# Five modulation vectors written to DRAM as rows turned by TensorE, and a later place for four of them

## The chip, the cores and the metric

The kernel runs on one core of one Trainium2 chip. Its time is the device time of an execution in microseconds; the figure used is the median of several runs.

## What is computed

The reference runs two blocks one after the other on a sequence of 512 tokens with 1024 channels, in float32.

```python
def first_block(x, c, ...):
    mod = silu(c) @ ada_w + ada_b
    shift, scale, gate = split(mod, 3)
    h = rms_norm(x, norm_pre_w) * (1 + scale) + shift
    z = h @ w_in                       # pooling branch and a gated linear recurrence (8 heads)
    y = concat([pool_out, hgrn_out]) @ w_out
    return x + gate * rms_norm(y, norm_post_w)

def second_block(x, c, ctx, c_ctx, ...):
    x, ctx = layer_norm(x), layer_norm(ctx)
    sh1, sc1, g1, sh2, sc2, g2 = split(silu(c) @ w_ada + b_ada, 6)
    # latents of context and sequence, rotary part, attention (8 heads), a 31-tap convolution
    y = concat([conv_out, attn_out]) @ w_o + b_o
    x_mid = layer_norm(ALPHA * x + g1 * y, ln1_g, ln1_b)
    f = conv_ffn(x_mid * (1 + sc2) + sh2, w_up, dw_w, dw_b, w_down, b_down)
    return layer_norm(ALPHA * x_mid + g2 * f, ln2_g, ln2_b)
```

What matters here is that some modulation vectors of length 1024 multiply or are added along the channels in a stage where the tokens lie on the partitions. There they are needed as a row that is repeated on all 128 partitions, while they are computed as columns: channel 128 j + p lies on partition p in column j of a 128x8 tile.

## The kernel before

The five engines each have a program of their own, written out in order, and wait for each other on named semaphores. The weights come as a stream of items through three buffers (RAW), which SP fetches. They are used in blocks numbered nb. For each block ScalarE casts the high part (WH, `split`), VectorE subtracts it for the low part (WL, `split`), and TensorE multiplies three times (high by high, high by low, low by high). There are four WH/WL pairs, so the cast of block nb + 4 can start only when TensorE has finished block nb, and every `split` in ScalarE's program is a place in a fixed queue: what stands before it holds it up. Some items of the stream are pieces of the modulation matrices instead; VectorE reduces them with its own dot operations ("dots") spread over the blocks.

The blocks around the change are: 32 to 53 for the pooling branch (with what is left of the recurrence), 54 to 71 for the output matrix of the first block (B_OUT = 54; 58 and 59 are the two small ones of the last pooling group, with out<-DH), 72 to 85 for the input matrix of the second block. Of these 76 is the rotary part of the latent, 77 to 79 are the query latent. Before block 67 TensorE transposes the context, and in blocks 68 to 71 it works token tile by token tile, so that it goes through all four blocks for each tile.

The vectors go through a DRAM tensor `vectors` of five rows (VEC). One is G1, the product of the first block's gate and norm_post_w. VectorE makes it ahead of block 54. ScalarE stores it after block 54's place in its program and two blocks later waits for that store and issues two loads that repeat the row on all partitions (G1R). The other four (M2[:, 16:24], BG, M2[:, 40:48] and BD) are made at block 62's place and stored by ScalarE at block 66's. Two of them are loaded again behind the attention (GOR, BOR), two ahead of the last matrix (ROWS). All stores are written with a DRAM access pattern in which consecutive elements of one partition are 128 elements apart. SP's queue holds the weight items, the first block's input in token order and, behind the item of block 67, the context (XC).

In TensorE's program PSUM tiles for small work come from four banks that are taken in turn (`take_aux`), each once its former tile has been read. An operation of TensorE that is a plain transpose is a matmul with the identity (IDN) as the moving operand.

In the profile's rows, the tile DH is a pooling tile, and PX holds the small column tiles, G1 and M2 among them. AT and KDT are the two halves of G1R, GP and HB hold the gates of the pooling branch, and PTA is scratch. Helpers record the operations, so L200 is every ScalarE copy, L207 every two-input VectorE operation, L186 every matmul, L194 every transpose, L182 and L183 every issue of a DMA.

Of the kernel before, what the change touches and what calls it, by code (L numbers as in the profile page):

```python
# [357 lines left out]
def build_in(nc, ctx, A, out, consts, masks):  # L358
# [30 lines left out]
    def col(name, j=0, n=1):  # L389
        return PC[:, COL[name] + j:COL[name] + j + n]  # L390
# [124 lines left out]
    def js(j):  # L515
        return slice(j * 128, (j + 1) * 128)
# [247 lines left out]
    def act_prog(e):  # L764
# [233 lines left out]
        def shifted(i):  # L998
# [3 lines left out]
            a.act(XLT[:, i, :], XLT[:, i, :], ACTF.Identity, bias=R3[:, i:i + 1], scale=R2[:, i:i + 1])\  # L1002
                .then_inc(S_.a_s, ("u", i))

        for nb in range(B_OUT, B_OUT + 14):
            if nb in (B_OUT + 9, B_OUT + 10):
                for i in range(2):
                    y_squares(2 * (nb - B_OUT - 9) + i, 0)
            if nb not in (B_OUT + 4, B_OUT + 5):
                split(nb + NW)  # L1010
            if nb == B_OUT:
                tail(0, 1)
                a.wait_ge(S_.v_s, "g1")
                a.dma(VEC[0].rearrange("(j p) -> p j", p=128), G1, True).then_inc(S_.vec, "g1", by=16)
            elif nb == B_OUT + 2:
                a.wait_ge(S_.vec, "g1")
                a.wait_ge(S_.p_sm, ("qs", 7))
                for c in range(2):
                    a.dma(G1R[c], VEC[0:1, 512 * c:512 * c + 512].partition_broadcast(128)).then_inc(S_.row, *["g1"] * c, by=16)
            elif nb in (B_OUT + 4, B_OUT + 5):  # L1020
                pool_mix(0, nb - B_OUT - 4, nb)
            elif nb in (B_OUT + 6, B_OUT + 7):
                i = nb - B_OUT - 6
                if i == 0:
                    a.wait_ge(S_.ctx, "ctx")
                    a.wait_ge(S_.v_h, ("mix", 1))
                    a.wait_ge(S_.v_s, ("ss", 7))
                a.wait_ge(S_.a_st)
                a.act(PTA[:, 0:D], XC[:, i, :], ACTF.Identity, scale=2.0 ** -10, acc=CST[:, i:i + 1]).then_inc(S_.a_st)
                a.wait_ge(S_.a_st)  # L1030
                a.act(PTA[:, 0:D], XC[:, i, :], ACTF.Square, scale=2.0 ** -5, acc=CST[:, 2 + i:3 + i])\
                    .then_inc(S_.a_st, ("cst", i))
            elif nb == B_OUT + 8:
                for i in range(2):
                    a.wait_ge(S_.v_s, "cm")
                    a.act(XC[:, i, :], XC[:, i, :], ACTF.Identity, bias=CST[:, 6 + i:7 + i], scale=CST[:, 4 + i:5 + i])\
                        .then_inc(S_.a_s, *["xcn"] * i)
            if nb in (B_OUT + 11, B_OUT + 12):
                for i in range(2):
                    a.wait_ge(S_.x[2 + i], "x2")  # L1040
                for i in ((0, 1) if nb == B_OUT + 11 else (2, 3)):
                    a.wait_ge(S_.a_st)
                    a.act(PTA[:, 0:D], XT2[:, i, :], ACTF.Identity, scale=2.0 ** -10, acc=MX[:, i:i + 1])\
                        .then_inc(S_.a_st, ("mx", i))
            if nb == B_OUT + 12:
                a.wait_ge(S_.v_ada, ("w_ada_2", 47, "c2"))
                a.wait_ge(S_.v_s, "bd")
                for n, cols in enumerate((M2[:, 16:24], BG, M2[:, 40:48], BD)):
                    a.dma(VEC[1 + n].rearrange("(j p) -> p j", p=128), cols, True).then_inc(S_.vec, *["g2"] * (n == 3), by=16)

        def ctx_tile(k):

# [67 lines left out]
        def latent(m):  # L1120

            split(77 + m + NW)
            a.wait_ge(S_.p_blk, 77 + m)
            a.copy(CQ[:, m, :], main.of(("cq", m))).then_inc(S_.a_ev, ("cq", m))
            a.wait_ge(S_.a_ev)
            if m > 1:
                a.wait_ge(S_.v_s, ("qa", 1))
            a.act(TMP[:, 512:1024] if m else TMP[:, 0:512], CQ[:, m, :], ACTF.Square).then_inc(S_.a_s, ("cqq", m))

        latent(0)  # L1130
        latent(1)
        for i, (lo, hi) in enumerate(((0, 512), (512, NKEY))):
# [223 lines left out]
    def dve_prog(e):  # L1356
# [215 lines left out]
        def with_dots(nb):  # L1572
            for t in range(4):
                for h, step in heads_at(nb, t) if nb < B_OUT else ():
                    hgrn(h, step)
                dots(nb, t)

        for h in range(2):
            mix_low(8 + h, XT[:, h, :])
        for nb in range(32, 36):  # L1580
# [18 lines left out]
            mix_low(8 + h, XT[:, h, :])  # L1599


        v.wait_ge(S_.v_ada, ("ada_w", 23, "c"))
        v.tt(G1, M1[:, 16:24], col("norm_post_w", 0, 8), MUL).then_inc(S_.v_s, "g1")

        def tile_done(name, i, h, first, second):

# [131 lines left out]
        def conv(place):  # L1738
            for j, k in CONV[place]:
                if k == 0:  # L1740
                    v.wait_ge(S_.v_ev, ("u2", j, 0))
                    op = v.ts(CV[:, j, :], VP[:, j, 0:S], col("conv_dw_w_2", j), col("conv_dw_b_2", j), MUL, ADD)
                else:
                    v.wait_ge(S_.v_cv, ("tap", j, k - 1))
                    op = v.stt(CV[:, j, :], VP[:, j, k:k + S], col("conv_dw_w_2", 4 * k + j), CV[:, j, :], MUL, ADD)
                op.then_inc(S_.v_cv, ("tap", j, k), *[("cv", j)] * (k == 30))
# [321 lines left out]
    def pe_prog(e):  # L2068
        pe = Eng(e)

        def take(name, at=None):
            bk = main.take(name, at)
            if main.before(name) is not None:
                pe.wait_ge(EV, main.before(name))
            return bk

        def take_aux(name, at=None):
            bk = aux.take(name, at)
            if aux.before(name) is not None:
                pe.wait_ge(AX, aux.before(name))  # L2080
            return bk
# [173 lines left out]
        def rows(bks, nb, xs, first, last, which=range(4), done=True):  # L2255

            wh, wl = WH[nb % NW], WL[nb % NW]
            pe.wait_ge(S_.v_w, nb)
            for q, (xh, xl, ready) in enumerate(xs):
                cs = slice(512 * q, 512 * q + 512)  # L2260
                pe.wait_ge(*ready)
                for i in which:
                    op = pe.mm3(bks[i], xh[:, js(i)], xl[:, js(i)], wh[:, cs], wl[:, cs], first and q == 0, last and q == 1)
            if done:
                op.then_inc(S_.p_blk, nb)
            return op
# [14 lines left out]
        def mixes(k):  # L2281
            return [(*mix_at(kk % 16), (S_.v_h, ("mix", kk % 16))) for kk in (k, k + 1)]

        ys = [take(("y", i, 0)) for i in range(3)] + [take_aux(("y", 3, 0))]
        at = aux.no[("y", 3, 0)]
        for n, k in enumerate((4, 6, 8, 2, 10, 12, 14, 0)):
            if n == 4:
                for m in range(2):
                    pool_mix(0, m, B_OUT + 4 + m)
            rows(ys, B_OUT + n + 2 * (n >= 4), mixes(k), n == 0, n == 7)  # L2290
        ys = [take(("y", 0, 1))] + [take_aux(("y", i, 1), (at + 4 - i) % 4) for i in (1, 2, 3)]
        for n in range(4):
            if n == 3:
# [54 lines left out]
        tiles(take(("kv", 1)), 75, hh, hl, (), 8)  # L2348
        tiles(take(("kr", 0)), 76, hh, hl, (), 8, part=False)
        tiles(take(("kr", 1))[:, 0:NCTX], 76, hch, hcl, (), 8)  # L2350

        def tick(k):
            if k == 1:
# [265 lines left out]
```

## Time and profile before

| | |
|---|---|
| median of 3 runs | 1203.27 us (1202.9 to 1203.66) |
| profiled execution | 1202.24 us |
| its span | 1200.4 us |
| mean granted clock of TensorE | 0.989 |
| TensorE matmul busy | 1142.4 us (95%) |
| VectorE busy | 859.1 us (72%) |
| ScalarE busy | 552.6 us (46%) |
| GpSimd busy | 159.9 us (13%) |
| DMA packets under 512 B | 7760 of 28307 |

The times in the rows are microseconds from the start of the span. A row of a timeline has the start, the duration, the engine, the line and operation, out<-in with shapes, and the count; where the engine stood idle before it, the length and what ended the wait stand in brackets. A matmul's end is modelled, so the distance between two starts tells more than its duration. "ACTq" and "SPq" rows are issues of DMAs by ScalarE and SP; they are no compute but take the queue's time.

### The profile page before, as it was taken

The page shows a single profiled execution, that of the slowest core. Times are in us where ns is not written, and L with a number is a line of the kernel's source. Part 1 is how long each engine was busy: PE and PEld are TensorE (multiplying, and loading weights), DVE is VectorE, ACT ScalarE, POOL GpSimd, SP SyncE. Part 2 cuts the span into 40 slices and gives each one's busy share as a digit, 9 for nine tenths or more (in the row PEclk, how much of TensorE's full clock was granted, in tenths as well). Part 3 has the DMA queues.
Part 4 walks back from the last instruction along what each step waited for, and adds up shares of the span by engine and source line. Part 5 has one row for each costly group of instructions (what it writes and reads, how often), then busy time and mean ns, then how long its engine had stood idle before and what let it go on. Part 6 is the DMA issues. An engine that isn't in the chain of part 4 may idle for free.

```text
span 1200.4 us, 14193 instructions
## 1 busy us (share of the span) xinstructions
PE 1142.4 (95%) x5548; PEld 932.2 (78%) x5548; DVE 859.1 (72%) x1346; ACT 552.6 (46%) x855; POOL 159.9 (13%) x179
## 2 busy tenths in 40 slices
PE   3979999999999999999999999998999999999996
PEld 2868888888788877888887766777888888888885
DVE  5788899999867783675789899586665656555236
ACT  4365545445623341776425665536544444442130
POOL 0044443244423200000100000100000000000001
PEclk9999999999999999999999999999999999999999
DMA  8833323323425576453111011111222322234201
GB/s 311 302 141 106 112 99 141 123 88 141 156 99 185 190 271 174 137 51 121 69 35 39 1 70 71 36 70 71 95 84 103 106 104 75 103 130 168 76 30 70
DMA packets 28307, 136.61 MB, mean 114 GB/s; under 512 B 7760, under 2 KB 8016, under 8 KB 14416
## 3 DMA queue, kind: packets, MB, share of 16 engines
q1 hardware_dynamic: 20448, 128.46, 30.6%
q10 hardware_dynamic: 7792, 7.25, 2.3%
q8 instruction: 44, 0.72, 0.3%
q14 instruction: 23, 0.19, 0.0%
HBM read 133.58 MB, written 2.12 MB: 113 GB/s over the span
## 4 chain that ended last, share of the span: by engine, by line
PE 58%; DVE 21%; ACT 8%; issue 5%; DMA 4%; POOL 3%; ACTq 0%; DVEq 0%; SPq 0%; POOLq 0%
PE PB L186 58%; DVE RAW L1382 3%; DVE WL L207 3%; ACT WH L200 3%; DVE CV L215 1%; DVE XL L215 1%; POOL PTA L207 1%; DVE AT L235 1%; DMA RAW<-in_wstream 1%; POOL UPA L207 1%; DVE SS L215 1%; DVE UPA L207 1%; DVE PTA L207 1%; DVE MPH L1382 1%; DMA XL<-in_xT 1%
## 5 line engine op out<-in xcount | busy, mean ns | idle before, releaser
L186 PE MATMUL PB<-HH,WH 128*128 128x512 f32 (+1 forms) x896 | 351.0, 392 | 4.6 <-DVE HL L207 1.7
L207 DVE TENSOR_TENSOR WL<-RAW,WH 128x1024 fp32r<-128x1024 f32 (+2 forms) x174 | 207.8, 1201 | 187.6 <-ACT WH L200 187.2
L186 PE MATMUL PB<-HH,WL 128*128 128x512 f32 (+1 forms) x896 | 341.5, 381 | 0.0
L186 PE MATMUL PB<-HL,WH 128*128 128x512 f32 (+1 forms) x896 | 340.7, 380 | 0.0
L200 ACT ACTIVATE WH<-RAW 128x1024 fp32r<-128x1024 f32 (+2 forms) x174 | 169.3, 979 | 298.6 <-PE PB L186 262.9
L186 PEld LDWEIGHTS PB<-HH,WH 128*128 128x128 f32 x896 | 170.1, 190 | 36.4 <-DVE HL L207 2.3
L186 PEld LDWEIGHTS PB<-HH,WL 128*128 128x128 f32 x896 | 169.6, 189 | 32.9
L186 PEld LDWEIGHTS PB<-HL,WH 128*128 128x128 f32 x896 | 170.0, 190 | 28.7 <-issue 0.5
L215 DVE SCALAR_TENSOR_TENSOR CV<-VP,PC,CV 128x512 f32<-128x512 f32 x120 | 86.7, 764 | 0.7
L207 POOL TENSOR_TENSOR PX<-PX,NPOW 128x2 f32<-128x2 f32 (+2 forms) x7 | 6.2, 891 | 483.4 <-DVE PX L207 437.1
L186 PE MATMUL PB<-WH,AH 128*128 128x512 f32 x176 | 68.5, 389 | 0.0
L186 PE MATMUL PB<-WL,AH 128*128 128x512 f32 x176 | 68.5, 389 | 0.0
L186 PE MATMUL PB<-WH,AL 128*128 128x512 f32 x176 | 68.5, 389 | 0.0
L1382 DVE CUSTOM_DVE_ANT_0 RAW<-RAW,CR,PC 128x1024 f32<-128x1024 f32 x48 | 63.5, 1341 | 0.0
L207 POOL TENSOR_TENSOR PTA<-HB 128x256 f32<-128x256 f32 (+1 forms) x53 | 46.6, 904 | 116.5 <-DVE HB L232 107.7
L201 ACT ACT_TABLE_LOAD x44 | 56.5, 1283 | 7.2 <-issue 6.5
L186 PE MATMUL PB<-WH,HH 128*128 128x512 f32 x128 | 53.5, 418 | 4.4 <-DVE WL L207 4.1
L186 PE MATMUL PB<-WL,HH 128*128 128x512 f32 x128 | 52.0, 406 | 0.0
L186 PE MATMUL PB<-WH,HL 128*128 128x512 f32 x128 | 51.6, 403 | 0.0
L207 POOL TENSOR_TENSOR UPA<-HB 128x256 f32<-128x256 f32 (+1 forms) x51 | 45.1, 908 | 44.9 <-DVE HB L232 39.9
L215 DVE SCALAR_TENSOR_TENSOR PTA<-PB,PC,PTA 128x511 f32<-128x511 f32 x66 | 49.2, 747 | 1.2
L186 PE MATMUL PB<-PTA,VG 128*128 128x512 f32 x96 | 49.3, 597 | 0.7 <-ACT PTA L201 0.6
(279 smaller groups left out, 1841.2 us busy)
## 6 DMA issues: line engine op xcount, KB each, us to landing
RAW<-in_wstream SPq DMA_DIRECT2D x108, 1024.0 KB, 4.8
RAW<-in_wstream SPq DMA_DIRECT2D x5, 768.0 KB, 4.2
RAW<-in_wstream SPq DMA_DIRECT2D x5, 512.0 KB, 3.4
XL<-in_xT SPq DMA_DIRECT2D x2, 1024.0 KB, 10.0
HB<-in_x SPq DMA_DIRECT2D x2, 1024.0 KB, 6.9
out<-XL SPq DMA_DIRECT2D x8, 256.0 KB, 2.0
ROWS<-in_rows ACTq DMA_DIRECT2D x3, 512.0 KB, 7.8
XC<-in_ctx SPq DMA_DIRECT2D x1, 1024.0 KB, 7.1
```

The source lines that it names most:

```text
L186: return self.put(lambda e: e.matmul(o, l, r, start=start, stop=stop, skip_group_check=skip))
L200: return self.put(lambda e: e.activation(o, i, f))
L201: return self.put(lambda e: e.activation(o, i, f, bias=bias, scale=scale))
L207: return self.put(lambda e: e.tensor_tensor(o, a, b, op))
L215: return self.put(lambda e: e.scalar_tensor_tensor(out=o, in0=a, scalar=s, in1=b, op0=o1, op1=o2))
L235: return self.put(lambda e: e.copy_predicated(o, mask, d))
L1382: v.put(lambda e: e.tensor_tensor_reduce(out=PROD if vec == "cc" else w, in0=w, in1=ROW[vec], scale=1.0, scalar=col(bias, j + i), op0=MUL, ...
```

## The change

The store of a vector with a scattered pattern is replaced by three steps: TensorE transposes the 128x8 columns into an 8x128 tile in PSUM, ScalarE copies it to SBUF, and the store writes 8 runs of 128 elements for each vector. G1's product is made ahead of block 32 in VectorE's program instead of ahead of block 54; its transpose stands behind TensorE's first output block, and its copy and store are where the store was. The four others are transposed behind block 76 and stored by ScalarE behind the cast of block 80, ahead of the query latent, in one DMA instead of four; their rows are gathered in the fourth tile of CV, so VectorE's convolution waits for the store before it first writes there.

```diff
@@ ScalarE's program
+        def vectors_out(name, n, rows, dst, done):
+            a.wait_ge(S_.p_sm, name)
+            a.copy(rows[0:8, 0:128 * n], aux.of(name)[0:8, 0:128 * n]).then_inc(S_.a_ax, name)
+            a.wait_ge(S_.a_ax, name)
+            a.dma(dst.rearrange("n (j p) -> j n p", p=128), rows[0:8, 0:128 * n].rearrange("j (n p) -> j n p", p=128))\
+                .then_inc(S_.vec, done, by=16)
+
             if nb == B_OUT:
                 tail(0, 1)
-                a.wait_ge(S_.v_s, "g1")
-                a.dma(VEC[0].rearrange("(j p) -> p j", p=128), G1, True).then_inc(S_.vec, "g1", by=16)
+                vectors_out("g1t", 1, DG, VEC[0:1], "g1")
...
-            if nb == B_OUT + 12:
-                a.wait_ge(S_.v_ada, ("w_ada_2", 47, "c2"))
-                a.wait_ge(S_.v_s, "bd")
-                for n, cols in enumerate((M2[:, 16:24], BG, M2[:, 40:48], BD)):
-                    a.dma(VEC[1 + n].rearrange("(j p) -> p j", p=128), cols, True).then_inc(S_.vec, *["g2"] * (n == 3), by=16)
...
+        vectors_out("g2t", 4, CV[:, 3, :], VEC[1:5], "g2")
         latent(0)
@@ VectorE's program
+        v.wait_ge(S_.v_ada, ("ada_w", 23, "c"))
+        v.tt(G1, M1[:, 16:24], col("norm_post_w", 0, 8), MUL).then_inc(S_.v_s, "g1")
         for h in range(2):
             mix_low(8 + h, XT[:, h, :])
...
-        v.wait_ge(S_.v_ada, ("ada_w", 23, "c"))
-        v.tt(G1, M1[:, 16:24], col("norm_post_w", 0, 8), MUL).then_inc(S_.v_s, "g1")
...
                 if k == 0:
+                    if j == 3:
+                        v.wait_ge(S_.vec, "g2")
@@ TensorE's program
+        def turned(name, *cols):
+            for n, z in enumerate(cols):
+                op = pe.tr(aux.of(name)[0:8, js(n)], z, IDN[:, :])
+            op.then_inc(S_.p_sm, name)
...
             rows(ys, B_OUT + n + 2 * (n >= 4), mixes(k), n == 0, n == 7)
+            if n == 0:
+                take_aux("g1t")
+                pe.wait_ge(S_.v_s, "g1")
+                turned("g1t", G1)
...
         tiles(take(("kr", 1))[:, 0:NCTX], 76, hch, hcl, (), 8)
+        take_aux("g2t")
+        pe.wait_ge(S_.v_ada, ("w_ada_2", 47, "c2"))
+        pe.wait_ge(S_.v_s, "bd")
+        turned("g2t", M2[:, 16:24], BG, M2[:, 40:48], BD)
```

## Rows read from the trace of the kernel before

**Rows 1.** The page's part 1: busy time, share of the span, instructions.

```profile
PE 1142.4 (95%) x5548; PEld 932.2 (78%) x5548; DVE 859.1 (72%) x1346; ACT 552.6 (46%) x855; POOL 159.9 (13%) x179
```

**Rows 2.** Waits of TensorE, 430 to 560: waiter, releaser, sum, times, longest.

```profile
PE PB L186 <- DVE WL L207: 3.5, 2, 2.1
PE PB L186 <- ACT CKV L200: 1.5, 1, 1.5
```

**Rows 3.** Timeline of TensorE at block 58, block 61 and block 71.

```profile
453.29 0.40 PE L186 MATMUL PB<-DH,WH 128*128 128x512 f32 x1
...
461.25 0.39 PE L186 MATMUL PB<-WH,HL 128*128 128x512 f32 x1
463.76 0.65 PE L186 MATMUL PB<-WH,HH 128*128 128x512 f32 x1 [2.13 <-DVE WL L207]
...
468.22 0.39 PE L186 MATMUL PB<-WH,HH 128*128 128x512 f32 x1
...
509.45 0.39 PE L186 MATMUL PB<-WH,HL 128*128 128x512 f32 x1
511.24 0.50 PE L186 MATMUL PB<-WH,HH 128*128 128x512 f32 x1 [1.40 <-DVE WL L207]
```

**Rows 4.** Windows of TensorE: stretch, length, busy (instructions), granted clock, DMA share, GB/s.

```profile
464.00:465.00 1.00, 1.00 (x3) 0.50 0.12 49
```

**Rows 5.** Timeline of ScalarE, 440 to 480.

```profile
448.05 0.39 ACTq L182 DMA_DIRECT2D vectors<-PX  x1
...
460.22 0.34 ACTq L183 DMA_DIRECT2D AT<-vectors  x1
460.58 0.76 ACTq L183 DMA_DIRECT2D KDT<-vectors  x1
461.39 1.06 ACT L200 ACTIVATE WH<-RAW 128x1024 fp32r<-128x1024 f32 x1 [11.46 <-issue]
```

**Rows 6.** Timeline of VectorE: G1, block 61's low half, two dots.

```profile
444.31 0.15 DVE L207 TENSOR_TENSOR PX<-PX,PC 128x8 f32<-128x8 f32 x1
...
462.48 1.23 DVE L207 TENSOR_TENSOR WL<-RAW,WH 128x1024 fp32r<-128x1024 f32 x1 [11.29 <-ACT WH L200]
...
471.89 1.28 DVE L1382 CUSTOM_DVE_ANT_0 RAW<-RAW,CR,PC 128x1024 f32<-128x1024 f32 x1
...
506.69 1.22 DVE L219 CUSTOM_DVE_ANT_0 HB<-HB 128x1024 f32<-128x1024 f32 x1
```

**Rows 7.** The critical chain, 430 to 800: start, length, what.

```profile
448.05 12.14 DMA vectors<-PX
...
474.01 7.13 DMA XC<-in_ctx
```

**Rows 8.** Timeline of ScalarE at the four other stores.

```profile
504.82 1.57 ACTq L182 DMA_DIRECT2D vectors<-PX  x2
...
506.42 2.40 ACTq L182 DMA_DIRECT2D vectors<-PX  x2
508.87 1.06 ACT L200 ACTIVATE WH<-RAW 128x1024 fp32r<-128x1024 f32 x1 [2.96 <-issue]
```

**Rows 9.** Groups of ScalarE by form: a copy from PSUM, count, busy, mean ns.

```profile
L200 ACT ACTIVATE KH<-PB 64x512 fp32r<-64x512 f32 x8 | 4.7, 592 | 2.8 <-PE PB L186 2.6
```

**Rows 10.** DMA issues of the page's part 6, and landing of the tensor vectors' DMAs.

```profile
out<-XL SPq DMA_DIRECT2D x8, 256.0 KB, 2.0
...
DMA to landing us min/median/max: 3.0/6.2/14.9
```

**Rows 11.** Timeline of TensorE at the transposes of the context.

```profile
498.33 1.91 PE L194 MATMUL PB<-IDN,XC 128*128 128x128 f32 x16
499.99 0.48 PE L186 MATMUL PB<-WH,MPH 128*128 128x512 f32 x1
```

**Rows 12.** Timeline of TensorE near block 32.

```profile
330.07 1.16 PE L186 MATMUL PB<-UPA 128*128 128x128 f32 x8 [1.29 <-DVE AT L235]
```

**Rows 13.** Timeline of ScalarE behind block 76.

```profile
573.44 1.06 ACT L200 ACTIVATE WH<-RAW 128x1024 fp32r<-128x1024 f32 x1 [5.97 <-PE PB L186]
580.22 1.06 ACT L200 ACTIVATE WH<-RAW 128x1024 fp32r<-128x1024 f32 x1 [5.72 <-PE PB L186]
```

## The prediction

> **What bounds the kernel now.** I began with the busy shares on the page [rows 1]. TensorE works for 95% of the span, so time is won only where TensorE stands still or runs at its lower clock. Next came the list of TensorE's own waits around the two places that the diff touches [rows 2]. It shows 3.5 us spent waiting for the low half of a weight block (DVE WL), in two waits. The timeline of TensorE places them [rows 3]: 2.13 us before 463.76 and 1.40 us before 511.24.
>
> The first wait costs more than its length. In regular running the matmuls start 0.227 us apart. The last one before the gap starts at 461.25, the first behind it at 463.76, so 2.51 - 0.23 = 2.28 us are lost. Behind the gap the granted clock is 0.50 (1.2 GHz) [rows 4], after TensorE had stood still for 2.13 us; by 468.22 it is back at the other level (2.4 GHz). From 463.76 to 468.22 there are 12 starts, in 4.46 us instead of 12 x 0.227 = 2.73 us, so 1.73 us more. Together this is **4.0 us**.
>
> Where it comes from is seen on ScalarE [rows 5]. It issues the store of G1 into the DRAM tensor at 448.05. It casts blocks 59 and 60, and then waits at the loads of G1R for the store to land. This takes until 460.2: the critical chain has the store as one piece of 12.14 us [rows 7]. Block 61's cast is queued behind and begins at 461.39. It could have begun when TensorE was done with block 57, which is when TensorE turns to the pool blocks (out<-DH), at 453.29 [rows 3]. VectorE makes the low half at 462.48 [rows 6], and TensorE starts at 463.76.
>
> The second wait: ScalarE issues four stores [rows 8], 1.57 us from 504.82 and 2.40 us from 506.42. The queue's own work takes this long because each of the four is scattered. Block 71's cast is behind them and begins at 508.87 instead of about 505.8, where TensorE is through with block 67 (18 matmuls of blocks 68 to 70 lie between that and 509.68, 18 x 0.227 = 4.1). TensorE's starts at 509.45 and 511.24 [rows 3] give 1.79 - 0.23 = **1.56 us** lost; no slow stretch follows.
>
> **The change, part by part.**
>
> *G1's store becomes rows.* TensorE transposes G1 behind block 54, which ends before 437, so ScalarE finds it ready. At 448.6, after tail(0,1), ScalarE copies 8x128 from PSUM and waits for its own copy. The nearest copy from PSUM, of four times the columns, takes 0.59 us [rows 9]; I take 0.3 for this one and 0.1 for the wait. The store is issued at about 449.1 with 8 runs of 512 B in place of 1024 elements of 4 B. Nothing in the trace is such a store. Its landing is bounded by the output's stores, 2.0 us for 256 KB [rows 10], and by the store that it replaces, 12.14 us [rows 7]. I take 3 us, since the runs of the former are the closer kind; a weight item is being loaded at that time. Then the wait of ScalarE ends at about 452, the two broadcast loads take 0.34 + 0.76 us of issuing [rows 5], and the cast of block 61 starts at 453.5. With 1.05 for the cast and 1.23 for the low half it is ready at about 456, and TensorE wants it at 461.5. So the store may land as late as 461.5 - 2.5 (cast, low half, signals) - 1.1 (issues) = 457.9 before TensorE waits: 8.8 us after it is issued. Gain 4.0.
>
> As a page on this: the Trainium skill's "DMA: Bandwidth & Descriptors" (the table of rules at its end) says that a non-contiguous last dimension becomes one descriptor per element and is to be rearranged, and its section on the anatomy of one DMA gives about 2 us as the fixed cost, most of it the receipt of the write. By that figure, as an estimate, the store would land near 451 and the gain would be the same 4.0; the 12.14 us of the scattered one agrees in kind [rows 7].
>
> *What is late next, between 461 and 511.* ScalarE and VectorE do the pool blocks 58 and 59 as soon as TensorE has them (455 to 462, from 463 to 470 before). The dots at 471.89 [rows 6] free the buffer behind which SP issues the context's load at 474.01 [rows 7]; they move ahead by about 8 us, and the load with them, landing near 473 instead of 481.14. ScalarE is then 4 us earlier against TensorE than before, on top of TensorE's own 4, so nothing that was in time becomes late.
>
> *Four stores leave ScalarE at 504.82.* Block 71's cast can start at 505.8 (old time), its low half is done by 508.1; VectorE is free for it at 507.84 at the latest, when its last dot ends [rows 6], which gives 509.1. TensorE wants it at 509.68. Gain 1.56, with a cover of 0.6 us; were VectorE's dots 1 us later, 0.4 of it would be lost.
>
> *Where these stores go.* Behind block 76 TensorE makes four transposes; ScalarE copies 8x512 (0.59 by the same row) and issues one store of 32 runs (0.4 to 1.6 us, the ends of the old issues). This stands between the cast at 573.44 and the one at 580.22, before which ScalarE has 5.72 us idle until TensorE is done with block 77 [rows 13]. It needs 0.6 + 0.1 + 1.6 = 2.3 at most: free, if the cover stays. The waits added: ScalarE waits for the transposes with latent(0) queued behind, about 0.6 us inside the same idle time; VectorE waits for the store before the first tap of conv j = 3, some 40 us later; the loads of GOR and BOR are at 767. A load of the weights by SP no longer shares the DMA engines with 4096 elements.
>
> *TensorE's new work.* 16 transposes with what follows take from 498.33 to 499.99 (next start) [rows 11], plus 0.08 for the wider step behind: 1.74 us, 0.11 each. So G1's single one costs 0.11 and g2's four 0.44. For coming in and going out of a small group I add 0.1 twice. Sum 0.75; bounds 0.52 (5 x 0.104, no edges) and 1.2 (each group pays once more the 0.27 us duration of a transpose). All of it is on the path: TensorE has no idle time after block 54 that it could use, once 463.76 is mended, and none behind 559.27. The banks of PSUM used after g1t and g2t shift by one; their former tiles were read long before, so no wait.
>
> *G1's product moves ahead of block 32.* One VectorE operation of 0.15 us [rows 6], now at about 326, where VectorE bounds: TensorE waits 1.29 us for it at 330.07 [rows 12]. Cost 0.15. At 444.31 it leaves VectorE where TensorE has no wait, so this gives nothing.
>
> **Sum:** -4.0 - 1.56 + 0.75 + 0.15 = **-4.7 us** (-4.9 to -4.2 by the bounds of TensorE's work). The profiled execution took 1202.24 us with a span of 1200.4. So 1195.7 of span and 1197.5 for the execution; the median of the runs is 1.03 above that execution, 1203.27, which gives **1198.6 us**.
>
> **Rivals.**
> (a) *The lower clock falls elsewhere.* An idle of 1.5 us near 559, behind ScalarE's copies of CKV [rows 2], passes at the full clock now. Moved by 5 us, it could be followed by a stretch like that of 463.76: 1.73 us. For: the fall there followed an idle not much longer. Against: the runs agree within 0.8 us. Result -4.7 + 1.7 = -3.0, 1200.3. The Trainium skill ("TensorE: Matmul & The Clock Gate", Part 1) says that the clock's decision runs free of the kernel, so such a shift is possible.
> (b) *The gain is given back.* If the context's load were still issued near 474 (SP's order, not the dots, holding it), ScalarE's chain would keep its time, and TensorE would start block 71 near 509.2 instead of 511.24: -2.0 + 0.9 = -1.1, 1202.2. Against: SP's issue follows the dots' end at 473.1 by 0.9 us.
> (c) *The change doesn't do what it says:* the store by rows lands after 8.8 us but before about 12, behind the weight load. Each us beyond 8.8 brings back 1 us of idle, and the clock's 1.73. At 10 us: -4.7 + 1.2 + 1.7 = -1.8, 1201.5.
> (d) *Slower.* The same store in eight streams behind the megabyte loads of SP, landing as late as the slowest DMA of this tensor now, 14.9 us [rows 10]: at 449.1 + 14.9 = 464.0, 3.8 later than now. TensorE would lose 4.0 + 3.8 at the first place: +3.8 - 1.56 + 0.9 = +3.1, 1206.4. It decides from a landing of about 12 us on. Against: the 256 KB stores land in 2.0 us.
>
> **Numbers.** Forecast 0.77, (a) 0.08, (b) 0.06, (c) 0.05, (d) 0.04. A measurement of this kernel tells 0.2%, 2.4 us, from no change. Faster: the forecast, (a), and a small part of (c): 0.85. Same: (b) and the rest of (c), 0.11. Slower 0.04. The range reaches 1.8 us below the forecast (TensorE's work at its lower bound, and up to 1 us if the idles at 511 to 560, which hang on ScalarE, shrink as well) and up to (a) with 0.5 us for the spread of the runs: 1196.8 to 1200.8.
>
> **What would show it.** Right: no idle of TensorE between 431 and the context's transposes; granted clock 1.0 throughout 440 to 500; the store of G1 landing within 4 us; the context's load issued near 466; no wait for WL at block 71; 5 more transposes of 0.27 us; a first difference between the traces of at most 0.4 us until block 54. Wrong: a wait of ScalarE for that store past 457.9, or a new half-clock stretch behind 500.

## The result, and the profile after

| | before | after |
|---|---|---|
| median of the runs | 1203.47 us (1202.9 to 1204.26, 4) | 1195.47 us (1194.97 to 1200.34, 4) |
| ratio, 95% interval | | 0.9941 (0.9921 to 0.996) |
| profiled execution, span | 1202.24, 1200.4 | 1200.34, 1198.5 |
| the same kernels timed again | 1202.31 (1199.34 to 1207.14, 12) | 1195.35 (1193.86 to 1197.98, 6) |

The change makes the kernel faster by 8.0 us; 4.7 were forecast, and 1195.47 lies 1.3 us below the low end of the range. The direction and the mechanism were right and the size was not. The profiled execution of after happened to be the slowest of its four, so its own time says little. The page of after, parts 1 and 3, to set beside [rows 1]:

```profile
PE 1142.8 (95%) x5553; PEld 932.8 (78%) x5553; DVE 859.4 (72%) x1346; ACT 553.8 (46%) x857; POOL 160.0 (13%) x179
...
DMA packets 23163, 136.61 MB, mean 114 GB/s; under 512 B 2576, under 2 KB 2872, under 8 KB 9272
```

TensorE has five instructions more (the transposes), ScalarE two (the copies). The same bytes go in 5144 fewer packets. The packets under 512 B fall from 7760 to 2576, by 5184; 5120 of these are the elements of the five scattered stores (5 x 1024).

TensorE's waits of after, 430 to 560 (waiter, releaser, sum, times, longest), which answer to [rows 2]:

```profile
PE PB L186 <- ACT CKV L200: 1.5, 1, 1.5
PE PB L194 <- ACT PTA L201: 0.9, 1, 0.9
PE PB L194 <- DVE XL L215: 0.8, 1, 0.8
PE PB L186 <- DVE HB L215: 0.6, 1, 0.6
```

The wait for WL, 3.5 us in two pieces before, is gone. The window of after at block 61 (stretch, length, busy of PE, PEld, DVE, ACT, POOL, granted clock, DMA share, GB/s) answers to [rows 4]:

```profile
460.00:465.00 5.00, 5.00 (x24) 4.14 (x23) 3.83 (x5) 1.76 (x3) 0.00 (x0) 1.00 0.45 177
```

TensorE is busy for all of it, at 2.4 GHz. ScalarE's timeline of after shows why, beside [rows 5]:

```profile
450.85 0.25 ACT L200 ACTIVATE DG<-PB 8x128 f32<-8x128 f32 x1
451.13 0.55 ACTq L183 DMA_DIRECT2D vectors<-DG  x1
451.72 1.37 ACT L200 ACTIVATE WH<-RAW 128x256 fp32r<-128x256 f32 x2 [0.62 <-ACT DG L200]
454.10 0.36 ACTq L183 DMA_DIRECT2D AT<-vectors  x1
454.48 0.45 ACTq L183 DMA_DIRECT2D KDT<-vectors  x1
455.58 1.06 ACT L200 ACTIVATE WH<-RAW 128x1024 fp32r<-128x1024 f32 x1 [2.49 <-PE PB L186]
```

The store of eight runs is issued at 451.13, and ScalarE goes on at 454.10. So it landed within 2.97 us (3 were taken; 12.14 before). Block 61's cast waits for TensorE and no longer for the store. TensorE is 2.08 us later at this point of the program than in the trace of before, of which 0.2 is the change's own work and 1.9 is not (below); less the 1.9 the cast starts at 453.7, where 453.5 was forecast.

The second place and the new place of the four vectors, ScalarE's timeline of after, beside [rows 8] and [rows 13]:

```profile
503.81 1.06 ACT L200 ACTIVATE WH<-RAW 128x1024 fp32r<-128x1024 f32 x1 [3.66 <-PE PB L186]
...
569.72 1.06 ACT L200 ACTIVATE WH<-RAW 128x1024 fp32r<-128x1024 f32 x1 [5.90 <-PE PB L186]
570.68 0.57 ACT L200 ACTIVATE CV<-PB 8x512 f32<-8x512 f32 x1
571.28 0.30 ACTq L183 DMA_DIRECT2D vectors<-CV  x1
576.95 1.06 ACT L200 ACTIVATE WH<-RAW 128x1024 fp32r<-128x1024 f32 x1 [5.70 <-PE PB L186]
```

Block 71's cast now has 3.66 us of idle time ahead of it. Behind block 76 the copy and the store take 0.9 us of an idle time of which 5.70 us remain.

**How the executions are compared.** TensorE runs the same matmuls in the same order in all these kernels, so the start of the n-th one in two traces can be subtracted; a step in that difference is a loss or a gain at that place. This table gives, for each traced execution, what TensorE lost ahead of and just behind block 61 and block 71. Its zero is the changed kernel: its three traces and that of the kernel with G1 alone agree there to 0.05 us, whatever else happened in them (4.04 us less than the first trace of before at block 61, 1.68 less at block 71).

| traced execution of the kernel before | time, us | idle before block 61 | lost there, clock included | idle before block 71 | lost there | both |
|---|---|---|---|---|---|---|
| the one of [rows 3] | 1202.24 | 2.13 | 4.0 | 1.40 | 1.7 | 5.7 |
| c_before | 1199.34 | 2.96 | 6.0 | 0 | 0 | 6.0 |
| c_before2 | 1200.26 | 2.9 | 5.9 | 0 | 0 | 5.9 |
| c_before3 | 1201.92 | 3.0 | 6.1 | 0 | 0 | 6.1 |
| c_before4 | 1200.58 | 3.03 | 6.1 | 0 | 0 | 6.1 |
| c_before5 | 1207.05 | 2.59 | 2.9 | 4.25 | 6.7 | 9.7 |
| c_before6 | 1203.97 | 3.02 | 4.9 | 1.77 | 3.7 | 8.6 |

The execution on which the prediction rested had the smallest loss of the seven. The mean is 6.9 us: 5.15 at block 61 and 1.72 at block 71. The changed kernel loses none of it and pays 0.6 for its transposes, so these traces account for 6.3 us of the 8.0.

The loss at block 71 goes with how long ScalarE's issue of the four stores takes, from the start of the first to the end of the last:

| traced execution | issue of the four, us | lost at block 71 |
|---|---|---|
| c_before4, c_before3, c_before, c_before2 | 2.42, 2.53, 2.76, 2.76 | 0 |
| the one of [rows 8] | 4.00 | 1.7 |
| c_before6 | 4.51 | 3.7 |
| c_before5 | 5.57 | 6.7 |

### The profile page after: what moved, and what is told of

Read it like the earlier page. It is cut to its first block, busy times and chain, and to the rows that moved or that the text cites. A ratio compares the mean times of both kernels' runs of the same rounds, so it can differ in the third digit from the quotient of the medians.

```text
span 1198.5 us, 14203 instructions
## 1 busy us (share of the span) xinstructions
PE 1142.8 (95%) x5553; PEld 932.8 (78%) x5553; DVE 859.4 (72%) x1346; ACT 553.8 (46%) x857; POOL 160.0 (13%) x179
## 2 busy tenths in 40 slices
DMA packets 23163, 136.61 MB, mean 114 GB/s; under 512 B 2576, under 2 KB 2872, under 8 KB 9272
## 4 chain that ended last, share of the span: by engine, by line
PE 64%; DVE 19%; ACT 6%; issue 4%; POOL 3%; DMA 3%; DVEq 0%; SPq 0%; ACTq 0%
PE PB L186 64%; DVE RAW L1385 3%; DVE WL L207 3%; ACT WH L200 2%; DMA RAW<-in_wstream 2%; DVE CV L215 1%; DVE XL L215 1%; DVE AT L235 1%; DVE UPA L207 1%; DVE SS L215 1%; POOL UPA L207 1%; POOL PTA L207 1%; DVE PTA L207 1%; DVE MPH L1385 1%; DMA XL<-in_xT 1%
```

## The experiments

No kernel here leaves out a part of the computation. A ratio is to the kernel before on the same chip, with its 95% interval.

**The two kernels again.** c_before and c_after are the kernel before and the changed one, without an edit.

> The kernel before, unchanged, as a yardstick for what varies by itself. Theory S (the 2.7 us by which the medians moved more than the traces account for are a matter of the first 50 us, whose clock varies from execution to execution): executions of this kernel scatter too, some 3 us below or above 1203, and a second profile shows another offset against the first before block 4, with the same two stalls of 2.1 and 1.4 us of TensorE behind it. Theory R (the scattered stores cost more in the timed executions than the two stalls of the profile): its times stay within 1202.5 to 1204.5.

> The changed kernel, unchanged. Its first profile began 2.1 us late against that of before, with half the clock from 33 to 47 us, and lost 1.3 us at half clock near 715. Theory S: a profile that starts like the one before has a span of 1195 to 1196.5, and the ratio of many runs comes out at about -5.3 us (0.9956). Theory R: the ratio stays at -7 to -8 us (0.9935 to 0.994), also for an execution that starts alike.

Measured: c_before 1202.31 (12 runs), 0.9997 (0.998 to 1.0015); c_after 1195.35 (6 runs), 0.9932 (0.991 to 0.9954). The gain repeats: 8.2 us against the 23 runs of before that were timed beside them (median 1203.57, from 1199.41 to 1206.75), 7.0 against the 12 of c_before. Neither theory holds whole. S was right that the kernel before scatters (three runs had lain within 0.8 us, these 23 lie over 7.3, and 35 on another chip over 12.0), and wrong on the ratio; R was right that the gain is 7 us or more, and wrong on the scatter.

**One part of the change alone.** G1 alone (its rows, its transpose, its earlier product; the four others left as scattered stores at block 66's place), and the four others alone.

```diff
@@ e_g1_only, against the changed kernel
+            if nb == B_OUT + 12:
+                a.wait_ge(S_.v_ada, ("w_ada_2", 47, "c2"))
+                a.wait_ge(S_.v_s, "bd")
+                for n, cols in enumerate((M2[:, 16:24], BG, M2[:, 40:48], BD)):
+                    a.dma(VEC[1 + n].rearrange("(j p) -> p j", p=128), cols, True).then_inc(S_.vec, *["g2"] * (n == 3), by=16)
...
-        vectors_out("g2t", 4, CV[:, 3, :], VEC[1:5], "g2")
...
-        turned("g2t", M2[:, 16:24], BG, M2[:, 40:48], BD)
@@ e_g2_only, against the changed kernel
-                vectors_out("g1t", 1, DG, VEC[0:1], "g1")
+                a.wait_ge(S_.v_s, "g1")
+                a.dma(VEC[0].rearrange("(j p) -> p j", p=128), G1, True).then_inc(S_.vec, "g1", by=16)
...
-                turned("g1t", G1)
```

> Only G1 goes by rows; the four others are stored scattered at block 66's place as before. By the terms of the prediction: the stall before block 61 and the slow stretch behind it go (-4.0), one transpose and the product's move cost 0.35: -3.7 us, and the wait of 1.4 us before block 71 stays if it hangs on the issues, or shrinks if it hangs on the context's load being early. Theory R: -5 or more.

> Only the four vectors go by rows, behind block 76; G1's store stays scattered and its stall of 2.1 us with it. By the terms: -1.56 + 0.55 = -1.0 us, and the two single changes sum to what both do together, -4.7 to -5.3. Theory R: -3 or more.

Measured: e_g1_only 1195.09 (6), 0.9929 (0.9906 to 0.9951), the same as the whole change. e_g2_only 1201.9 (12), 0.9981 (0.9963 to 0.9999). In the trace of the latter TensorE loses 6.7 us at block 61 (the scattered store lands after 13.1 us, the idle time is 3.63 us) and nothing at block 71. Against 1203.57 that is 8.5 us for G1 alone, where 3.7 were expected, and 1.7 for the four others, where 1.0 was. The two don't add up: the whole change gains no more than G1 alone.

So G1 alone brings the second gain too, though the four scattered stores still stand where they stood. ScalarE's timeline of e_g1_only:

```profile
496.33 1.01 ACTq L182 DMA_DIRECT2D vectors<-PX  x2
...
497.38 1.46 ACTq L182 DMA_DIRECT2D vectors<-PX  x2
501.23 1.06 ACT L200 ACTIVATE WH<-RAW 128x1024 fp32r<-128x1024 f32 x1 [3.81 <-PE PB L186]
```

The issues take 2.5 us and hurt nobody, since ScalarE then has 3.81 us to spare before block 71. Together that is room for 6.3 us of issuing, more than the longest seen, 5.57. It is that early because the context's load is issued at 465.62 and not at 474.01 [rows 7]. The second loss thus needed two things at once: a context that came late, which G1's wait had made, and issues that took 4 us or more. By this room, to remove either is enough. e_g2_only shows no loss at block 71 either, but neither do four of the seven traces of before, so its one trace doesn't prove it.

**The wait or the form?** G1's scattered store with time enough to land: the product ahead of block 32, the store ahead of block 48's recurrence. In the second kernel the four others are stored behind block 76, scattered as before. Neither has a transpose.

```diff
@@ e_g1_early_scattered, against the kernel before
         for p, nb in ((2, 36), (1, 42), (0, 48)):
+            if p == 0:
+                a.wait_ge(S_.v_s, "g1")
+                a.dma(VEC[0].rearrange("(j p) -> p j", p=128), G1, True).then_inc(S_.vec, "g1", by=16)
@@ e_all_scattered_moved, on top of it
-            if nb == B_OUT + 12:
...
+        a.wait_ge(S_.v_ada, ("w_ada_2", 47, "c2"))
+        a.wait_ge(S_.v_s, "bd")
+        for n, cols in enumerate((M2[:, 16:24], BG, M2[:, 40:48], BD)):
+            a.dma(VEC[1 + n].rearrange("(j p) -> p j", p=128), cols, True).then_inc(S_.vec, *["g2"] * (n == 3), by=16)
         latent(0)
```

> G1's product ahead of block 32 and its scattered store, unchanged in form, issued at block 48's place, about 50 us ahead of the wait; the four others as before; no transposes. Theory W (all of the gain is that ScalarE no longer waits for that store): the stall and slow stretch before block 61 are gone as with the rows, the second stall too since the context's chain is early; 1195 us like G1 alone by rows, 0.15 faster by the transpose. Theory F (the form matters, for 1024 elements of 4 B hinder the weight loads wherever they are): slower than G1 by rows by over 2 us, with waits for RAW near block 48.

> As the run before, and the four others scattered too, but issued behind block 76, where the rows' store of the changed kernel is: no transposes at all, 4 us of issuing in a gap of 5.7 us. Theory W: 0.6 us faster than the changed kernel (no transposes: 0.1 at block 54, 0.46 behind block 76), 1194.8. Theory F: slower than it, with a wait of TensorE for block 81's low half near 580.

Measured: 1204.59 (12), 1.0 (0.9982 to 1.0018), and 1206.01 (12), 1.0003 (0.9983 to 1.0023). Both are as slow as before, although in both the waits for WL at blocks 61 and 71 are gone and the 4.04 and the 1.68 us come back there. They are lost at a new place. Of e_g1_early_scattered, ScalarE's timeline:

```profile
414.38 0.39 ACTq L182 DMA_DIRECT2D vectors<-PX  x1
...
430.01 1.06 ACT L200 ACTIVATE WH<-RAW 128x1024 fp32r<-128x1024 f32 x1 [8.85 <-DMA RAW<-in_wstream]
```

its view of the tile RAW (the buffers of the weight stream), 405 to 460, last line, and TensorE's waits, 400 to 440:

```profile
DMA to landing us min/median/max: 2.9/5.8/12.7
```

```profile
PE PB L186 <- DVE HB L215: 6.9, 1, 6.9
```

Nobody waits for the store. But the weight item that is being loaded beside it takes 12.7 us (in the same stretch of after none takes over 7.5), ScalarE waits 8.85 us for it, TensorE 6.9, and 4.9 us at 1.2 GHz follow. By the difference of the matmuls' starts 8.6 us are lost between 430 and 455. In the second kernel the same load takes 12.8 us, and 9.0 are lost. Its four stores behind block 76 hold up a load too, which lands after 16.8 us, but cost TensorE nothing that the difference shows (no step between 560 and 600). So theory F came true for G1's store, and not for the four others: a load that is held up costs time only where its item is needed soon. In e_g1_only, too, the load beside the four stores takes 16.9 us, and TensorE loses nothing.

This was foreseen by no step of the prediction: **the scattered store holds up the megabyte loads beside it**, not only the engine that waits for it.

**Half of it.** Columns 0 to 3 of G1 stored early, 4 to 7 at the old place.

```diff
@@ e_g1_half, against the kernel before
+                a.dma(VEC[0, 0:512].rearrange("(j p) -> p j", p=128), G1[:, 0:4], True).then_inc(S_.vec, by=16)
...
-                a.dma(VEC[0].rearrange("(j p) -> p j", p=128), G1, True).then_inc(S_.vec, "g1", by=16)
+                a.dma(VEC[0, 512:1024].rearrange("(j p) -> p j", p=128), G1[:, 4:8], True).then_inc(S_.vec, "g1", by=16)
```

> Half of G1's columns stored scattered at block 48's place, the other half where the store was, so 512 elements are waited for instead of 1024. If the landing goes with the number of elements it is 6 to 7 us, inside the 8.8 us that TensorE's cover allows: no idle before block 61 and 1195 to 1196 us. If it has a large fixed part (12 us whatever the number) the stall stays and the time is near 1203.

Measured: 1210.97 (12), 1.0047 (1.0025 to 1.0069), slower than before. Neither 1195 nor 1203 came out. 512 elements do all that 1024 do: the load beside the early half takes 13.8 us and TensorE stands still for 8.0 us. That half lands after 11.4 us; the second, issued at 454.38, after 11.75 us, at 466.13. The time does not go with the number of elements. By the starts of the matmuls 8.9 us are lost ahead of block 54, 0.5 at block 61 and 5.6 at block 71: behind the first stall TensorE is so late that ScalarE's wait for the second half hardly matters at block 61, but the context's load is issued only at 480.05, and the four stores then stand in the way of block 71.

**Neither the wait nor the rows: the store alone.** To the changed kernel one more store of G1 is added, into a DRAM tensor of its own, right behind the row store. Nothing waits for it until 760. In e_extra_dense its elements lie side by side as in the kernel before; in e_extra_apart each of the 1024 lies at the start of a 512-byte row of its own. The diff is that of the former; in the latter SCR has the shape [D, 128] and the store goes to SCR[:, 0].

```diff
@@ against the changed kernel
+    SCR = nc.dram_tensor("extra", [D], F32).ap()
...
                 vectors_out("g1t", 1, DG, VEC[0:1], "g1")
+                a.dma(SCR.rearrange("(j p) -> p j", p=128), G1, True).then_inc(S_.extra, by=16)
...
         a.wait_ge(S_.p_sm, ("o", 7, 5))
+        a.wait_ge(S_.extra)
```

> The changed kernel with the old scattered store added back right behind the store by rows, into a DRAM tensor of its own and waited for only behind the attention. If the wait is the whole cost (theory W), same as the changed kernel within 0.5 us. If a scattered store holds up the DMAs beside it (theory F), the packets of 8 KB of the weight loads take over 2 us again, the loads of G1R and the cast of block 62 come late, and the kernel loses 2 to 6 us.

> As the run before, but each of the 1024 elements goes to a row of its own, 512 B apart. If the elements hinder each other because neighbours in DRAM come from different partitions, it lands within 3 to 5 us and disturbs nothing: same as the changed kernel. If the number of small writes is what counts, it is as slow as the dense one.

Measured: e_extra_dense 1200.91 (12), 0.9984 (0.9972 to 0.9997); e_extra_apart 1197.61 (11), 0.9955 (0.994 to 0.997). These two ran on another chip than c_after, where the kernel before has a median of 1202.9 and not 1203.57, so their distance from c_after is given by medians and by ratios. ScalarE's timeline of e_extra_dense:

```profile
451.23 0.40 ACTq L182 DMA_DIRECT2D extra<-PX  x1
...
466.61 1.06 ACT L200 ACTIVATE WH<-RAW 128x1024 fp32r<-128x1024 f32 x1 [8.27 <-DMA RAW<-in_wstream]
```

The last line of its view of the tile RAW, 405 to 460, and below it that of e_extra_apart:

```profile
DMA to landing us min/median/max: 3.0/4.8/14.0
```

```profile
DMA to landing us min/median/max: 3.0/4.9/7.5
```

The dense store takes back 5.6 us by the medians (1200.91 against 1195.35) and 6.3 by the ratios, as theory F expected. By the starts of the matmuls it is 1.1 us at block 62, whose weights came late, and 4.4 at block 65, whose cast stands in ScalarE's program behind the context's statistics: the context's load is issued at 475.69 here and at 468.19 in after. The dense store itself lands after 10.4 us, and the first load of G1R beside it takes 14.2 us and not 4.6. The store with its elements apart lands after 4.2 us and loses nothing at either place. Its median is 2.3 us above c_after all the same (2.8 by the ratios). Its trace is 1.0 us longer than c_after's, and 0.9 of that is there before 100 us, long before the store; whether the rest of the medians' distance is a cost is open.

The records of the DMA packets say the same. A packet of 8192 B of the weight stream usually takes 0.31 us. Behind the first 60 us of the span these many took over 2 us:

| kernel | scattered dense stores | packets over 2 us |
|---|---|---|
| before, seven traces | 5 | 59 to 76 |
| e_g1_half | 6, two of them with 512 elements | 85 |
| e_g1_early_scattered | 5 | 67 |
| e_all_scattered_moved | 5 | 32 |
| e_g1_only | 4 | 38 |
| e_g2_only | 1 | 33 |
| e_extra_dense | 1, not waited for | 35 |
| e_extra_apart | 1, elements 512 B apart | 4 |
| changed kernel, three traces | 0 | 0 |
| e_g2_early (below) | 0 | 0 |

The four of e_extra_apart took 2.00 to 2.05 us; the longest of the changed kernel took 1.66.
In the first trace of before the 1024 packets of G1's store all start between 450.85 and 451.93 and are recorded at 9 ns each, and yet the store has landed only at 460.2. The packets of 8192 B beside it take up to 3.7 us, up to 9.9 us in e_extra_dense.

As a page on this: the Trainium skill's "DMA: Bandwidth & Descriptors" (Specifications) gives 512 B as the least transfer for the line rate and says that below it the DMA engines read, modify and write. e_extra_apart, with just as many elements under 512 B and hardly a delay, shows that the size alone isn't it. What matters is that they lie densely in DRAM. Whether elements in the same few hundred bytes hinder each other, or all of them in the same 4 KB, was not tried, and the mechanism inside was not measured.

**The place of the four others.** The changed kernel with its four rows made early: transposed ahead of TensorE's work on the context, copied into DG and stored at block 66's place, where the scattered stores were.

```diff
@@ e_g2_early, against the changed kernel
             if nb == B_OUT + 12:
+                vectors_out("g2t", 4, DG, VEC[1:5], "g2")
...
         for n in range(4):
+            if n == 2:
+                take_aux("g2t", at)
+                pe.wait_ge(S_.v_ada, ("w_ada_2", 47, "c2"))
+                pe.wait_ge(S_.v_s, "bd")
+                turned("g2t", M2[:, 16:24], BG, M2[:, 40:48], BD)
```

> The changed kernel with the four vectors transposed ahead of block 66 and stored by rows at block 66's place, where the scattered stores were. The store's issue is one of 0.5 us instead of four with 4 us, and ScalarE has 3.7 us idle before block 71's cast in the changed kernel: nothing lost, same as the changed kernel within 0.3 us. Rival (the place behind the rotary latent is worth the 1.6 us of the second stall): 1.5 us slower, with a wait for WL before block 71.

Measured: 1201.79 (12), 0.9979 (0.9959 to 0.9999), 6.4 us above c_after by the medians and 5.7 by the ratios (another chip again). TensorE's waits of e_g2_early, 430 to 560:

```profile
PE PB L194 <- ACT DG L200: 2.6, 1, 2.6
...
PE PB L194 <- ACT XR L198: 1.3, 1, 1.3
```

and ScalarE's copy of the rows:

```profile
497.02 0.57 ACT L200 ACTIVATE DG<-PB 8x512 f32<-8x512 f32 x1
```

Here no low half comes late and nothing at block 71 waits. Of the four banks for small work the only one free for these rows is one that the context's transposes need soon after. TensorE waits 1.3 us until ScalarE has read the bank's former tile, and 2.6 us more at the context, until ScalarE has copied the rows, at 497.02: the copy stands at block 66's place in its program, 9 us behind the transposes. So 4.7 us are lost between 475 and 509 (the four transposes included, which are then missing behind block 76); the remaining 1 us or more of the medians' distance isn't seen in the trace. Both expectations missed. The later place matters, but not for the issues of the stores: it is a bank that is held until ScalarE comes to the copy in its queue.

**Does the loss at these two places go with the time of an execution?** Both kernels without an edit, one profiled execution each.

> The kernel before once more, one look. Its two traces so far lost 4.0 + 1.6 and 6.0 + 0.0 us before blocks 61 and 71 and came out at 1202.2 and 1199.3, both below the median of 1203.6 of its 35 executions. If the place before block 61 carries what the medians moved beyond the prediction, another execution shows a landing of 12 to 14 us and 4 to 8 us lost there, and its time goes with that.

> As the run before: the loss before block 61 lies between 4 and 8 us. If instead the executions differ in the first 100 us or behind 700, the loss before block 61 is 4 to 6 us again and the rest of the gain stays open.

> One more traced execution of the kernel before. If its time is above 1203.6, the loss before blocks 61 and 71 together is 8 us or more (the slow executions are slow there); the rival is 6 us there and the rest in half-clock stretches in the first 100 us or behind 700.

> As c_before4. Over the traced executions of before, the time goes with the loss before blocks 61 and 71 if that is the cause; by the rival it goes with what is lost in other stages.

> As c_before4: above 1203.6 with 8 us or more lost before blocks 61 and 71, or with 6 us there and the rest in other stages.

> A third trace of the changed kernel: no idle of TensorE between 431 and the context's transposes, no packet of a weight load over 2 us behind 60 us, 1194 to 1198 us; with a slow start like that of its first trace 1200.

Measured: 1200.26, 1201.92, 1200.58, 1207.05, 1203.97, and 1194.33 for the changed kernel; the losses stand in the table above. The two executions of before that are above its median are those with 8.6 and 9.7 us lost; the other five lost 5.7 to 6.1. The times less these losses still lie from 1193.3 to 1197.4, so other places scatter as much as these two. Of c_before5, TensorE's timeline:

```profile
463.33 0.50 PE L186 MATMUL PB<-WH,HH 128*128 128x512 f32 x1 [2.59 <-DVE WL L207]
...
512.07 0.79 PE L186 MATMUL PB<-WH,HH 128*128 128x512 f32 x1 [4.25 <-DVE WL L207]
```

its ScalarE's timeline:

```profile
504.09 1.46 ACTq L182 DMA_DIRECT2D vectors<-PX  x2
...
505.58 4.08 ACTq L182 DMA_DIRECT2D vectors<-PX  x2
509.70 1.06 ACT L200 ACTIVATE WH<-RAW 128x1024 fp32r<-128x1024 f32 x1 [4.53 <-issue]
```

and its windows behind the two places:

```profile
513.00:514.00 1.00, 1.00 (x4) 0.71 (x3) 0.17 (x1) 1.00 (x5) 0.00 (x0) 0.50 1.19 25
464.00:465.00 1.00, 1.00 (x6) 0.82 (x5) 0.36 (x1) 1.00 (x2) 0.00 (x0) 1.00 0.74 131
```

Here the issues of the four stores took 5.5 us and not 4.0 [rows 8], and TensorE stood still for 4.25 us before block 71. Behind it the starts come slowly for 4.8 us (11 of them), at 1.2 GHz. Behind block 61, after 2.59 us of idle time, the clock was 2.4 GHz in this execution; in c_before, after 2.96 us, 14 starts come at 1.2 GHz, in 6.0 us instead of 3.2; in the one of [rows 4], after 2.13 us, 12 in 4.46, of which 9 are slow. In c_before6, after 3.02 us of idle time, the first five come at 2.4 GHz and the next nine at 1.2. So such a stall costs about its own length, or up to 2.9 us more.

The rest of the scatter is seen in both kernels. In the first 100 us the seven traces of before differ by up to 2.0 us, the three of the changed kernel by up to 3.6. At 705 to 711 some lose 1.3 to 1.6 us, and others differ by 1.0 us near 775 and 1.5 near 822. Windows of after at two of these places:

```profile
706.00:707.00 1.00, 1.00 (x3) 0.33 (x1) 1.00 (x3) 0.51 (x2) 0.00 (x0) 0.50 0.00 0
40.00:45.00 5.00, 5.00 (x17) 4.32 (x18) 4.80 (x10) 1.38 (x2) 0.00 (x0) 0.50 0.82 306
```

That is why its profiled execution took 1200.34. It is 1.7 us late at 100 us, most of it from 39 to 42, at half clock, which the trace of before enters only at 40.7; 0.2 more come at a wait near 427, and 1.3 at 706, at half clock.

## Why the prediction was right in kind and too small

- **The first term, -4.0, is the step that failed.** The mechanism held (the store's landing, ScalarE's wait, block 61's cast, and half clock behind the stall). The size was that of one execution. Seven show 2.9 to 6.1 us there, with a mean of 5.15, and e_g2_only 6.7. The landing varied little (12.1 to 13.1 us); the clock's share behind it did, from nothing to 2.9 us. That makes 1.15 of the 3.3 us by which the forecast was too small.
- **The second term, -1.56,** has a mean of 1.72 over the seven, so its size was fair, but it is 0 in four of them and 3.7 and 6.7 in two. Its cause was half told. The prediction put it down to the issues, and it does go with their length; e_g1_only shows that with the context's load early they are harmless. That an issue takes long "because each of the four is scattered" is also only half of it: the one of G1 is scattered too and takes 0.39 us. So G1 is worth nearly the whole gain, and the move of the four others nothing that e_g1_only (1195.09) against c_after (1195.35) would show. That their move without G1 removes this term is likely, but e_g2_only's one trace doesn't show it, as said.
- **The range left out what would have covered this.** It took in the bounds of TensorE's new work and a clock that falls elsewhere, but not that the profiled execution may be a mild one, though it had two stalls whose price depends on the clock. With 2.9 to 6.1 and 0 to 6.7 for the two terms it would have reached down past 1195. The three timed runs, 0.8 us apart, made the kernel look steadier than the 7.3 us of 23 runs.
- **"No longer shares the DMA engines with 4096 elements"** stood there as a remark with no price. It was the place to ask what such a store does to the loads beside it. e_extra_dense puts 5.5 us on it in its trace. Since the prediction removed these stores anyway, its sum had the stall and with it most of this; but the reason given, that ScalarE waits, is only a part. Moving the wait alone would have gained nothing (e_g1_early_scattered).
- **Right by their numbers:** the landing of the row store (3 forecast, 2.97 at most; the 2 us that the prediction cites beside it, from the Trainium skill's "DMA: Bandwidth & Descriptors", stand in a section on DMAs that GpSimd issues, and ScalarE issued this one). The copy, 0.25 us for 0.3. The context's load, at 468.19 less 1.9 us, 466.3, where "near 466" stood:

```profile
468.19 0.38 SPq L183 DMA_DIRECT2D XC<-in_ctx  x1
```

- The four transposes and their edges: the starts of the matmuls move by 0.45 us between 572 and 580 in every kernel that has them there, and by 0 in e_g1_only; 0.54 was forecast. G1's: 0.10 to 0.15 between 430 and 455, where 0.21 was forecast. The earlier product, 0.15 forecast, costs at most 0.1. Together 0.6 for 0.9. No new stall behind 500, and no wait for WL. Two slips in the working change nothing: block 67 ends at 505.6 (509.68 - 4.1) and not 505.8, and the upper bound of TensorE's new work is 1.3 by its own terms (0.75 + 2 x 0.27) and not 1.2.
- **The rivals.** (a) didn't occur: in none of the 18 traces does the clock fall between 525 and 700, though the idle of 1.46 us near 559 is in all of them. Half clock appears at 706 in the profiled execution of after, a sign of being wrong by the prediction's last lines, but an execution of before has it too (c_before5, at 711), so it isn't the change's. (b) and (c) fall with the two times above. (d), the loss through a late landing, doesn't occur for rows. What comes nearest is a weight load that lands late behind a scattered store; that made e_g1_half slower than before.
- **Open.** The traces account for 6.3 us; the medians give 7.0 (against c_before) to 8.2, so 0.7 to 1.9 us have no place. The seven traced executions of before have a mean of 1202.2, against medians of 1202.3 to 1204.4 of the timed ones, so they may be a mild sample once more; seven are too few to say so. What makes the issue of two scattered stores take 1.0 us in one execution and 4.1 in another wasn't tried, and why the clock answers a stall of 2.6 us or of 3.0 so differently can't be told from these traces.

## What to carry to other kernels

When a term of the sum is a stall with half clock behind it, its size in one trace is a draw: give it a range from its bare length up to what the slow stretch adds at its longest, and let the range of the forecast follow. A small store whose elements are scattered over partitions and dense in DRAM is to be counted as a transfer that can hold up the load beside it by 5 us and more, not as its bytes; before moving the wait for it, ask which load lies beside it and how soon its data are needed, and if TensorE can turn the tile for a few tenths of a us, turn it. When two stalls lie on one chain, check whether mending the first mends the second, before both fixes are built.

## What the runs showed of the hardware

- A store of 1024 single 4-byte elements from 128 partitions, dense in DRAM, lands in 10.4 to 13.1 us when it is alone of its kind; 512 elements take 11.4 and 11.75. Four such stores in a row land after 9.1 to 20.2 us. A store of the same 4 KB as eight runs of 512 B lands within 3.0.
- While one of them lands, a 1 MB load beside it takes 12.2 to 14.0 us instead of at most 7.6 in the same stretch of the changed kernel, and its packets up to 9.9 us instead of 0.31. Beside four, a load takes 14.0 to 18.4 us. With the same 1024 elements 512 B apart the store lands in 4.2 us, the load takes at most 7.5 and the longest packet 2.05.
- ScalarE's issue of two such stores takes 1.0 to 4.1 us, and that time varies from execution to execution. One store of all four vectors by rows is issued in 0.30 us.
- A standstill of TensorE of 2.1 to 3.0 us is followed by no slow stretch, or by 9 to 14 matmul starts at 1.2 GHz, in different executions of the same kernel.
